# Output units two to four as seven block products each, with the sums on VectorE

## The reference, cut to what matters

```python
ya = einsum('bte,ed->btd', oa * silu(ua), w_a_out)      # 512 -> 1024
yb = einsum('bte,ed->btd', ob * silu(ub), w_b_out)      # 512 -> 1024
mixed = sigmoid(ga) * ya + sigmoid(gb) * yb
y = x + einsum('btd,de->bte', mixed, w_o)               # 1024 -> 1024
```

## Time and profile before

| | us |
|---|---|
| median of 3 runs | 523.32 (523.22 to 523.72) |
| the profiled execution, its own time | 523.65 |
| its span in the trace | 521.9 |
| busy in the span: PE, DVE, ACT, POOL | 515.1, 370.7, 258.2, 76.7 |

### The profile page before, as it was taken

One profiled execution on the slowest core, in us unless ns is written; L12 is line 12 of the kernel. 1 busy time (PEld: TensorE's weight loads), 2 busy tenths in 40 slices (PEclk: granted clock), 3 DMA queues, 4 the chain that ended last, 5 costly groups with the idle time before them and its releaser, 6 DMA issues.

```text
span 521.9 us, 10124 instructions
## 1 busy us (share of the span) xinstructions
PE 515.1 (99%) x4188; PEld 485.5 (93%) x4188; DVE 370.7 (71%) x718; ACT 258.2 (49%) x434; POOL 76.7 (15%) x73
## 2 busy tenths in 40 slices
PE   8999999999999999999999999999999999999997
PEld 6889999999998988989998888999999999999997
DVE  5878758899979989478857668563987556665331
ACT  7655764344366566864244665653566532231100
POOL 3506000014034314284000000000000000000000
PEclk9999999999999999999999999999999999999999
DMA  7623305142331322023230016020232172245111
GB/s 274 266 80 123 92 1 167 35 168 82 117 133 28 140 82 82 1 82 122 87 113 4 1 47 212 2 82 1 82 105 98 42 252 80 82 162 189 50 52 46
DMA packets 15359, 50.45 MB, mean 97 GB/s; under 512 B 2288, under 2 KB 6000, under 8 KB 11728
## 3 DMA queue, kind: packets, MB, share of 16 engines
q1 hardware_dynamic: 15168, 49.49, 27.6%
q10 hardware_dynamic: 144, 0.30, 0.2%
HBM read 42.82 MB, written 6.82 MB: 95 GB/s over the span
## 4 chain that ended last, share of the span: by engine, by line
PE 91%; DVE 4%; issue 2%; ACT 2%; DMA 1%; ACTq 0%
PE PS L665 40%; PE PS L1004 9%; PE PS L958 8%; PE PS L989 8%; PE PS L619 4%; PE PS L784 3%; PE PS L765 3%; PE PS L649 3%; PE PS L869 2%; PE PS L741 2%; PE PS L710 2%; PE PS L849 1%; PE PS L690 1%; PE PS L598 1%; PE PS L793 1%
## 5 line engine op out<-in xcount | busy, mean ns | idle before, releaser
L665 PE MATMUL PS<-xhi,whi 128*128 128x272 f32 x320 | 94.6, 296 | 0.0
L665 PE MATMUL PS<-xlo,whi 128*128 128x272 f32 x320 | 92.4, 289 | 0.0
L665 PE MATMUL PS<-xhi,wlo 128*128 128x272 f32 x320 | 92.1, 288 | 0.0
L1452 DVE TENSOR_TENSOR wlo<-raw,whi 128x2048 fp32r<-128x2048 f32 (+1 forms) x31 | 64.5, 2080 | 17.3 <-ACT whi L1051 15.9
L665 PE MATMUL PS<-whi,xhi 128*128 128x256 f32 x256 | 73.4, 287 | 0.8 <-DVE nmx L1844 0.8
L665 PE MATMUL PS<-wlo,xhi 128*128 128x256 f32 x256 | 72.4, 283 | 0.0
L665 PE MATMUL PS<-whi,xlo 128*128 128x256 f32 x256 | 71.9, 281 | 0.0
L665 PEld LDWEIGHTS PS<-xhi,whi 128*128 128x128 f32 x320 | 60.3, 189 | 2.9 <-issue 2.3
L1051 ACT ACTIVATE whi<-raw 128x2048 fp32r<-128x2048 f32 (+1 forms) x31 | 52.1, 1682 | 18.2 <-PE PS L1004 18.2
L665 PEld LDWEIGHTS PS<-xhi,wlo 128*128 128x128 f32 x320 | 60.4, 189 | 0.0
L665 PEld LDWEIGHTS PS<-xlo,whi 128*128 128x128 f32 x320 | 60.2, 188 | 0.0
(11 more groups left out here) (283 smaller groups left out, 1318.2 us busy)
## 6 DMA issues: line engine op xcount, KB each, us to landing
raw<-in_w_units SPq DMA_DIRECT2D x28, 1024.0 KB, 4.9
raw<-in_w_mixes SPq DMA_DIRECT2D x8, 512.0 KB, 3.4
stage<-in_x_kw_qi SPq DMA_DIRECT2D x7, 564.5 KB, 5.1
res<-in_x_kw_qi SPq DMA_DIRECT2D x1, 2176.0 KB, 8.1
out<-res SPq DMA_DIRECT2D x16, 136.0 KB, 1.7
out<-vals SPq DMA_DIRECT2D x2, 1024.0 KB, 6.2
out<-kT SPq DMA_DIRECT2D x1, 1088.0 KB, 8.7
out<-tm SPq DMA_DIRECT2D x1, 1024.0 KB, 8.0
```

The source lines that it names most:

```text
L665: mm = pe.matmul(out, lhsT, rhs, start=(k == 0), stop=(k == 23))
L1452: dve.tensor_tensor(wlo[:, uu % 2, 0:n], raw[:, uu % 2, 0:n], whi[:, uu % 2, 0:n].bitcast(F32), ALU.subtract).then_inc(w_lo, 1)
```

## The change

Output unit out0 stays a direct product. Units out1, out2 and out3 become seven block products of 12 matmuls each (`out(o)`), 84 matmuls in place of 96.

- The input blocks are pairs of chunks of `mixed`: (0, 2), (1, 3), (4, 6), (5, 7). For each pair VectorE forms four sums of 272 columns (`sums_m`), ScalarE their high parts (`sums_high`), VectorE their low parts (`sums_low`): 16 of each. VectorE's lie in mix rounds 2 to 6 and after round 7.
- The weight sums of each of the three units are three VectorE instructions of 1024, 512 and 512 columns (`out_sums`); their parts are four high and four low instructions (`out_high`, `out_low`) of 512, 1024, 1024 and 1024 columns.
- The low part of out0's weights (2048 columns) moves from round 6 to round 1 (`out0_lo`), its high part to round 0, its load ahead of mix2's.
- out1's load waits for `out0_lo` and stands in SP's list ahead of mix4's, with out1's high and low parts later. Both halves of `raw` are given out anew (`half_of`): mix units all in half 0, out0 in half 1.
- The residual is loaded in four parts of two chunks (`load_res`), each behind a wait on the sums.
- Every unit's products are read by VectorE alone (`out_added`), seven a unit in place of four. PE waits for such a read before the next product on that bank.
- The two multiplications of a mix round wait for a branch each (`mix_done` counts both).

The diff, cut to its core:

```diff
+UNITS += [("out0", "out")] + [(f"out{_o}", "last") for _o in range(1, D // UC)]
...
+M_LOWS = [(k, n) for k in (0, 1) for n in M_FORMS] + [(k, n) for n in M_FORMS for k in (2, 3)]
+M_AT = {v: k + 1 for k, v in enumerate(M_LOWS)}
+OUT_BANKS = [{"a": 4, "b": 5, "c": 6}, {"a": 0, "b": 1, "c": 2}]
+DIRECT_TAKEN = [(None, 0, 0), (None, 0, 1), (None, 1, 0), (None, 1, 1)]
+TAKEN_ORDER = [("p1", 0, 0), ("p5", 1, 1), ("p6", 1, 0), ("p3", 1, 0), ("p7", 1, 1), ("p2", 0, 0), ("p4", 0, 1)]
+OUT_SLOT = {1: 0, 2: 1, 3: 0}
+OUT_RAW = {0: 1, 1: 1, 2: 0, 3: 1}
...
         ohi_b = by(PAIRS, sb_at("ohi_b", PAIRS * NT, F32R, at_bias)[:, :])
         olo = by(2 * PAIRS, sb_at("olo", 2 * PAIRS * NT, F32R, at_o)[:, :])
...
+        def half_of(buf, uu):
+            n, kind, d = unit_cols(uu), UNITS[uu][1], UNITS[uu][0][3:]
+            if kind == "mix":
+                return buf[:, 0, n * (int(d) % 2):n * (int(d) % 2 + 1)]
+            if kind in ("out", "last"):
+                return buf[:, OUT_RAW[int(d)], :]
+            return buf[:, uu % 2, 0:n]
...
+            def load_out(o):
+                uu = U[f"out{o}"]
+                if o == 0:
+                    sp.wait_ge(f_lo_done, len(PARTS) * len(FAST))
+                elif o == 1:
+                    sp.wait_ge(out0_lo, 1)
+                elif o == 2:
+                    sp.wait_ge(w_lo, direct_index(U["mix7"]) + 1)
+                else:
+                    sp.wait_ge(y_lo_done, len(PARTS))
+                sp.dma_start(half_of(raw, uu), w_units[big_index(uu)]).then_inc(out_raw[o], 16)
+            def load_res(o):
+                sp.wait_ge(ms_summed, len(M_FORMS) * (o + 1))
+                e = UC // P * o
+                sp.dma_start(res[o], x_kw_qi.rearrange("c p n -> p c n")[:, e:e + UC // P, 1:FIRST_AT]).then_inc(out_res[o], 16)
...
             sp.wait_ge(bias_done, 1)
             for r in range(4):
                 sp.dma_start(bias_r[32 * r:32 * r + 32, :], bias_s[0:DEC, :]).then_inc(bias_rep, 16)
-            for name, _ in UNITS[U["gate2"]:]:
+            for name, _ in UNITS[U["gate2"]:U["mix2"]]:
                 load_unit(name)
-                if name == "mix2":
-                    sp.wait_ge(f_done, len(PRODUCTS) * len(FAST))
-                    sp.dma_start(res, x_kw_qi.rearrange("c p n -> p c n")[:, :, 1:FIRST_AT]).then_inc(res_in, 16)
-            for g in range(2 * KC):
-                e, h = divmod(g, 2)
-                sp.wait_ge(y_out, g + 1)
-                sp.dma_start(y_fm[:, e, halved(h)], res[:, e, halved(h)]).then_inc(st_y, 16)
+            load_out(0)
+            load_unit("mix2")
+            load_unit("mix3")
+            load_out(1)
+            load_unit("mix4")
+            load_unit("mix5")
+            load_res(0)
+            load_unit("mix6")
+            load_unit("mix7")
+            load_res(1)
+            load_out(2)
+            load_res(2)
+            load_res(3)
+            load_out(3)
...
+            def out(o):
+                banks = OUT_BANKS[o % 2]
+                for n, form, block_, b in PRODUCTS:
+                    part = [form in p for p in PARTS].index(True)
+                    pe.wait_ge(y_lo_done, len(PARTS) * (o - 1) + (0, 2, 3, 1)[part] + 1)
+                    if n == "p1":
+                        if o >= 2:
+                            pe.wait_ge(y_added, taken_by(o - 1, -1))
+                        else:
+                            pe.wait_ge(mix_used, D // P)
+                    elif n in ("p5", "p2") and o >= 3:
+                        pe.wait_ge(y_added, taken_last(o - 2, "p3" if n == "p5" else "p2"))
+                    elif n == "p6":
+                        pe.wait_ge(y_added, taken_last(o, "p1"))
+                    elif n == "p3":
+                        pe.wait_ge(y_added, taken_last(o, "p5"))
+                    elif n == "p7":
+                        pe.wait_ge(y_added, taken_last(o, "p6"))
+                    elif n == "p4":
+                        pe.wait_ge(y_added, taken_last(o, "p7"))
+                    opens = n in ("p1", "p5", "p2")
+                    for c in range(KC // 2):
+                        if o == 1 and block_ in M_FORMS:
+                            pe.wait_ge(ms_low, M_AT[(c, block_)])
+                        for k, (a, w) in enumerate(PASSES):
+                            q = QUARTER * FORMS[form]
+                            wt = by(KC // 2, (slots_hi, slots_lo)[w][OUT_SLOT[o]][:, q:q + QUARTER])
+                            mm = pe.matmul(ps[:, banks[b], 0:HALF_NT], wt[:, c, :], m_block(a, block_, c),
+                                           start=(opens and c + k == 0), stop=(c == KC // 2 - 1 and k == 2),
+                                           skip_group_check=True)
+                    mm.then_inc(y_done, 1)
+            for o in range(1, OUTS):
+                out(o)
...
-                        act.wait_ge(mix_done, int(d) + 1)
-                    else:
-                        act.wait_ge(y_done, 4 * (int(d) + 1))
-                n = unit_cols(uu)
-                act.activation(whi[:, uu % 2, 0:n], raw[:, uu % 2, 0:n], ACT.Copy).then_inc(w_hi, 1)
...
+            def out_high(o, part):
+                uu = U[f"out{o}"]
+                first, slot = PARTS[part][0], OUT_SLOT[o]
+                q, n = QUARTER * FORMS[first], QUARTER * len(PARTS[part])
+                if part == 0:
+                    act.wait_ge(out_raw[o], 16)
+                    if o == 1:
+                        act.wait_ge(f_done, len(PRODUCTS) * len(FAST))
+                    else:
+                        act.wait_ge(y_done, product_at(o - 1, 0))
+                if first in QUAD:
+                    src = half_of(raw, uu)[:, QUARTER * QUAD[first]:QUARTER * QUAD[first] + n]
+                else:
+                    act.wait_ge(yt_done, 3 * (o - 1) + (1 if first == "t1" else 3))
+                    src = slots_t[slot][:, q:q + n]
+                act.activation(slots_hi[slot][:, q:q + n], src, ACT.Copy).then_inc(y_hi_done, 1)
+            def sums_high(these):
+                for k, form in these:
+                    act.wait_ge(ms_summed, summed_at(k, form))
+                    act.activation(m_block(0, form, k), m_sum(form, k), ACT.Copy).then_inc(ms_high, 1)
...
-                w_high(f"mix{d + 2}" if d + 2 < D // P else f"out{d + 2 - D // P}")
-            for o in range(2, D // UC):
-                w_high(f"out{o}")
+                if d + 2 < D // P:
+                    w_high(f"mix{d + 2}")
+                if d == 0:
+                    act.wait_ge(out_raw[0], 16)
+                    act.activation(half_of(whi, U["out0"]), half_of(raw, U["out0"]), ACT.Copy).then_inc(out0_hi, 1)
+                elif d == 3:
+                    out_high(1, 0)
+                    out_high(1, 3)
+                elif d == 4:
+                    sums_high(M_LOWS[0:4])
+                elif d == 5:
+                    sums_high(M_LOWS[4:8])
+                elif d == 6:
+                    out_high(1, 1)
+                    out_high(1, 2)
+            sums_high(M_LOWS[8:])
+            for o in range(2, OUTS):
+                for part in (0, 3, 1, 2):
+                    out_high(o, part)
...
+            def sums_m(k):
+                for form, a, b, op in (("s1", m_raw(0, k, 1), m_raw(1, k, 1), ALU.add),
+                                       ("s2", m_sum("s1", k), m_raw(0, k, 0), ALU.subtract),
+                                       ("s4", m_raw(1, k, 0), m_sum("s2", k), ALU.subtract),
+                                       ("s3", m_raw(0, k, 0), m_raw(0, k, 1), ALU.subtract)):
+                    if form in ("s2", "s4"):
+                        dve.wait_ge(ms_summed, summed_at(k, form) - 1)
+                    elif form == "s1":
+                        dve.wait_ge(m_lo, K_HALVES[1][k] + 1)
+                    dve.tensor_tensor(m_sum(form, k), a, b, op).then_inc(ms_summed, 1)
+            def sums_low(these):
+                for k, form in these:
+                    dve.wait_ge(ms_high, M_AT[(k, form)])
+                    dve.tensor_tensor(m_block(1, form, k), m_sum(form, k), m_block(0, form, k).bitcast(F32),
+                                      ALU.subtract).then_inc(ms_low, 1)
...
+            def out_sums(o):
+                uu, slot = U[f"out{o}"], OUT_SLOT[o]
+                dve.wait_ge(out_raw[o], 16)
+                if o == 1:
+                    dve.wait_ge(f_done, len(PRODUCTS) * len(FAST))
+                else:
+                    dve.wait_ge(y_done, product_at(o - 1, 0))
+                w = half_of(raw, uu)
+                t = {n: slots_t[slot][:, QUARTER * FORMS[n]:QUARTER * (FORMS[n] + 1)] for n in ("t1", "t2", "t4")}
+                both = slots_t[slot][:, QUARTER * FORMS["t1"]:QUARTER * (FORMS["t1"] + 2)]
+                dve.tensor_tensor(both, w[:, QUARTER:3 * QUARTER], w[:, 0:2 * QUARTER], ALU.subtract).then_inc(yt_done, 1)
+                dve.wait_ge(yt_done, 3 * o - 2)
```

(130 more changed lines are left out.)

42 lines of the change are left out of this document (24 added, 18 removed).

## The result

The changed kernel takes 527.32 us (527.17 to 528.17, 4 runs) against 523.52 us for the kernel before beside it (523.22 to 523.81): ratio 1.0076, 95% interval 1.0058 to 1.0093. It is slower by 3.8 us, forecast was 3.1. The profiled execution went from 523.65 to 527.21 us, its span from 521.9 to 525.5.

What follows compares the result with a forecast made beforehand. PE (TensorE), busy 99% of the span, was taken as the bound. The terms -4.5 - 1.3 + 3.3 + 1.4 + 2.0 + 1.4 + 0.8 gave +3.1 us, from 523.32 to 526.4 us, range 524.0 to 528.6.

Steps and rivals of the forecast that it cites:

- Matmuls and the old gap: On PE, 36 fewer matmuls save 4.5 us; writing out0's low weights earlier removes a gap, 1.09 + 0.13 + 0.08 = 1.3 us.
- The load of mix4: In the mix stage, mix4's load is served behind out1's, which waits for out0's low part; mix4 starts 3.3 us later.
- rival 2: Mix stage: mix4's load is not held by out1's, its wait is 1.1, total 524.2 us; chance 10%.
- VectorE's rounds: Mix stage: VectorE's rounds of 6.6, 6.6, 6.3 us exceed PE's 6.02; mix5 to mix7 wait 0.56, 0.56, 0.31, +1.4 us.
- Rival 3: The clock falls in PE's wait before mix4, adding 1.5 us to the sum, total 528 us; chance 10%.
- list of signs: What would show it: PE's waits, load times, 4152 matmuls; wrong if the granted clock leaves 1.00, among other conditions.
- The output stage: PE waits for VectorE's additions: p6 of out1 +2.0 us, p3 of out1 +1.4, p3 of out2 +0.8.
- Prices: On VectorE, a 272-column sum takes 0.44 us, with 0.35 as the lower bound.
- rival 1: Small VectorE instructions are cheap, 0.30 us for 272 columns, so the kernel ends faster, at 521.8 us; chance 7%.
- rival 4: Semaphore waits cost VectorE its overlap, 0.08 us more for each, new waits 13.3, total 530.8 us; chance 7%.

Runs made afterwards that it cites:

- e1: The changed kernel with SP issuing mix4's load ahead of out1's: 523.43 us, ratio 0.9995 to the kernel before.
- e4: The changed kernel with mix4's load ahead of out1's, but issued only after out0's low part is written: 524.54 us, ratio 1.0013 to the kernel before.
- e8: The changed kernel with 22 extra matmuls, their result overwritten, filling PE's wait before mix4: 527.23 us, ratio 1.0066 to the kernel before.
- e6: The changed kernel with the twelve sums of the first three pairs on GpSimd, load and read order unchanged: 525.21 us, ratio 1.0027 to the kernel before.
- e7: The kernel of e6 with 22 extra matmuls, their result overwritten, filling PE's wait before mix4: 524.07 us, ratio 1.0006 to the kernel before.
- e2: The changed kernel with VectorE's output-stage list reordered, bank-freeing additions ahead of the next unit's weight sums: 523.86 us, ratio 1.0006 to the kernel before.
- e3: The changed kernel with the edits of both e1 and e2: 520.29 us, ratio 0.9938 to the kernel before.
- e5: The kernel of e3 with the twelve sums of the first three pairs moved from VectorE to GpSimd: 518.56 us, ratio 0.9900 to the kernel before.

## Why the prediction was right

Point by point, by its own terms:

- **Matmuls and the old gap**, -4.5 and -1.3: 36 matmuls fewer are in the trace (4152 for 4188), and no wait for out0's weights is left. One term of the gap was read wrongly: the 0.13 us from the weights to the first matmul lies inside the 1.09 already. What belongs there is that a matmul starts before the one in front of it ends:

```profile
469.32 0.29 PE L989 MATMUL PS<-olo,whi 128*128 128x272 f32 x1
```

The next started at 470.70, 1.38 later in place of 0.13, and with the slow first one the gap cost 1.3. This term came out right by luck.

- **The load of mix4**, +3.3: measured 3.3, by the forecast chain: issue of out1's load at 440.36 (440.1), mix4 landed 5.9 us after its issue (5.6), start at 449.05 (448.7). e1 and e4 show both parts of the cause, and rival 2 (not held) is out.
- **VectorE's rounds**, +1.4 in three waits: with the clock kept, in e8, mix5 to mix7 come 0.56, 0.56 and 0.31 late, as forecast. In the changed kernel's profiled execution this step did not happen as told. There were no waits, because the clock fell: mix4 took longer, and VectorE's weights were ready in time for mix5 to mix7. The loss of the four units was 1.75 us beyond 24.10.
- **Rival 3**, the fallen clock: it had 10%, and the clock fell in two of four executions. Its own price was right (1.5 us by e6 and e7), the way it was added was wrong: the prediction put 1.5 us on top of the sum, but the fall and the late VectorE cover each other, and it adds 0.1 us or less (25.85 against 25.79). By its own list of signs the prediction was wrong here, for the granted clock left 1.00. That the total held all the same was luck in the executions in which the clock fell; in the two in which it did not, the time was the same, and e8 shows the forecast terms at work with the clock kept.
- **The output stage**, +2.0, +1.4, +0.8: from the starts 491.66, 494.60 and 506.00 and 0.1255 us a matmul between them, the losses are 1.7, 1.4 and 0.9. All three are the order of VectorE's list (e2), not its amount.
- **Prices**: 0.43 to 0.44 us for a sum of 272 columns, from 0.44; rival 1 (cheap small instructions) is out. VectorE's instructions start before their forerunner's end also with satisfied waits (p5's addition at 494.06 behind the sum of 493.45 + 0.69 = 494.14), so rival 4 is out.

The sum by these measured terms is -4.5 - 1.3 + 3.3 + 1.75 + 1.7 + 1.4 + 0.9 = +3.3 us; the profiled executions differ by 3.56. 0.2 of the difference lies before the stage: mix0 starts at 421.66 and not at 421.44. Whether that is an effect of out0's earlier load or chance is open.

## What to carry to other kernels

Less arithmetic on the bounding engine pays only as far as the lists of the other engines, and of the DMA queue, keep it fed: here 4.5 us of matmuls were given back twice over by one load placed ahead of a more urgent one, by rounds of VectorE longer than TensorE's, and by additions placed behind work that was wanted later. Before adding work to a second engine, write its list out against the first engine's due times, and put what frees a buffer ahead of what prepares the next unit. A cost found beside a wait is not to be added to it unseen: a slower clock and a late engine can cover each other, and only a run without one of them tells.

## What the runs showed of the hardware

- **The clock fell after a wait of 3.1 to 3.3 us**, and had not after 1.6 and 1.1. It shows behind this wait in the profiled executions of the changed kernel, e2 and e6, but two of the changed kernel's four executions and three of e2's twelve had a mean clock of 1.00: it need not fall each time.
- **It can fall without such a wait.** In e3's profiled execution it fell early in the program: two windows, TensorE first, the clock before the last two numbers.

```profile
24.00:26.00 2.00, 2.00 (x7) 1.64 (x8) 0.25 (x3) 0.00 (x0) 1.58 (x4) 0.76 0.12 45
26.00:28.00 2.00, 2.00 (x6) 1.40 (x5) 1.90 (x1) 0.83 (x2) 0.07 (x1) 0.50 0.00 0
```

TensorE had waited 0.58 us at 22.7 and then had ten matmuls of two columns; what let the clock fall there is open. It means that the mean clock of an execution without a trace does not say where the clock fell.
- **GpSimd and VectorE slow each other.** In e6, VectorE's weight sums of 512 columns beside GpSimd's sums: start, length, what.

```profile
473.33 1.15 DVE L2196 TENSOR_TENSOR slot_t<-raw,slot_t 128x512 f32<-128x512 f32 x1
474.52 1.16 DVE L2199 TENSOR_TENSOR slot_t<-raw,slot_t 128x512 f32<-128x512 f32 x1
```

They took 0.69 us in the changed kernel. Three of GpSimd's four sums of 272 columns in the same stretch, the first beside VectorE's sum of 1024 columns, the last beside VectorE reading PSUM:

```profile
472.24 1.69 POOL L2399 TENSOR_TENSOR ms_sum<-wk,gates_v 128x272 f32<-128x272 f32 x1 [15.97 <-DVE xlo L2249]
474.01 1.11 POOL L2399 TENSOR_TENSOR ms_sum<-ms_sum,wk 128x272 f32<-128x272 f32 x1
...
476.27 0.77 POOL L2399 TENSOR_TENSOR ms_sum<-wk 128x272 f32<-128x272 f32 x1
```

A sum takes 0.77 alone, and 1.1 to 1.7 beside an instruction of VectorE with two SBUF inputs. The Trainium skill, page "SBUF — State Buffer", section "Who interferes with whom", says that a VectorE instruction with two SBUF inputs contends with a GpSimd instruction that reads SBUF; by that rule the trace agrees, with VectorE's 512-column sums longer by 0.5 us each and GpSimd's by 0.3 to 0.9. It came to some 0.9 us on VectorE in that round; in e5 it left TensorE without a listed wait.
